# Two attentions dealt out pair by pair between weight products: a two-network kernel on one core

## The reference, cut to what matters

```python
h = rms_norm(x, norm_mix_pre[i])
z = h @ w_in[i]
c_q, c_kv, k_rope, q_c, k_c, v_c, g_a, g_b, g_c = jnp.split(z, split_points, axis=-1)
o_a = mla_attention(c_q, c_kv, k_rope, positions, ...)      # latent attention: 8 heads, all 512 keys
o_b = fourier_mix(h)
o_c = windowed_gqa(q_c, k_c, v_c, positions, gqa_sink[i])   # grouped: 8 heads, 3 key blocks of 128
merged = (jax.nn.sigmoid(g_a) * (o_a @ w_branch_a[i])
          + jax.nn.sigmoid(g_b) * (o_b @ w_branch_b[i])
          + jax.nn.sigmoid(g_c) * (o_c @ w_branch_c[i]))
x = x + rms_norm(merged @ w_out[i], norm_mix_post[i])
```

## Time and profile before

| | us |
|---|---|
| median of 3 runs (3287.8 to 3292.09) | 3291.27 |
| the profiled execution: time | 3288.2 |
| the profiled execution: span of its trace | 3286.4 |
| PE busy in the span | 3092.7 (94%) |
| DVE / ACT / POOL busy | 1221.0 / 1294.7 / 1495.4 |
| grouped attention, layer 0 and 1 | 51.3, 49.9 |
| latent attention, layer 0 and 1 | 70.3, 70.4 |

### The profile page before, as it was taken

One profiled execution on the slowest core, in us unless ns is written; L12 is line 12 of the kernel. 1 busy time (PEld: TensorE's weight loads), 2 busy tenths in 40 slices (PEclk: granted clock), 3 DMA queues, 4 the chain that ended last, 5 costly groups with the idle time before them and its releaser, 6 DMA issues.

```text
span 3286.4 us, 42020 instructions
## 1 busy us (share of the span) xinstructions
PE 3092.7 (94%) x15048; PEld 2487.2 (76%) x15048; DVE 1221.0 (37%) x2009; ACT 1294.7 (39%) x2023; POOL 1495.4 (46%) x879
## 2 busy tenths in 40 slices
PE   8989998999989989998999989879999998899999
PEld 6856676888867856686888769757788886688887
DVE  5345433221053445434221060443455215645510
ACT  3353543322243353543223243454555326344421
POOL 3366444444444456355444453343444433344443
PEclk9999999999999999999999989989999998899999
DMA  3212132233322213032333312101332322223332
GB/s 124 90 46 89 40 103 83 95 96 96 103 84 84 90 36 99 21 121 77 96 97 102 100 61 101 64 1 52 95 97 96 94 92 74 74 91 97 97 93 90
DMA packets 78522, 274.37 MB, mean 83 GB/s; under 512 B 8504, under 2 KB 12216, under 8 KB 78400
## 3 DMA queue, kind: packets, MB, share of 16 engines
q1 hardware_dynamic: 74064, 266.05, 25.8%
q10 hardware_dynamic: 4336, 6.63, 0.6%
HBM read 270.54 MB, written 2.10 MB: 83 GB/s over the span
## 4 chain that ended last, share of the span: by engine, by line
PE 83%; DVE 7%; ACT 4%; issue 3%; POOL 2%; DMA 1%; DVEq 0%; ACTq 0%; SPq 0%; POOLq 0%
PE ps L583 24%; PE ps L584 23%; PE ps L585 23%; PE ps L810 2%; PE ps L820 2%; DVE HL L1583 1%; PE ps L841 1%; PE ps L944 1%; PE ps L945 1%; PE ps L946 1%; PE ps L659 1%; DVE ps L1572 1%; DVE X L1575 1%; POOL WLO L2026 1%; ACT SG L1269 1%
## 5 line engine op out<-in xcount | busy, mean ns | idle before, releaser
L2026 POOL TENSOR_TENSOR WLO<-WRAW,WHI 128x1024 fp32r<-128x1024 f32 x471 | 1139.2, 2422 | 1338.4 <-ACT WHI L1110 1337.6
L583 PE MATMUL ps<-HH,WHI 128*128 128x512 f32 x2288 | 905.4, 396 | 47.2 <-DVE HL L1583 23.5
L585 PE MATMUL ps<-HH,WLO 128*128 128x512 f32 x2288 | 898.4, 393 | 0.0
L584 PE MATMUL ps<-HL,WHI 128*128 128x512 f32 x2288 | 898.2, 393 | 0.0
L1110 ACT ACTIVATE WHI<-WRAW 128x1024 fp32r<-128x1024 f32 x471 | 494.7, 1052 | 400.8 <-DMA WRAW<-wall 400.8
L583 PEld LDWEIGHTS ps<-HH,WHI 128*128 128x128 f32 x2288 | 434.0, 190 | 155.9 <-POOL WLO L2026 21.9
L585 PEld LDWEIGHTS ps<-HH,WLO 128*128 128x128 f32 x2288 | 434.0, 190 | 92.4
L584 PEld LDWEIGHTS ps<-HL,WHI 128*128 128x128 f32 x2288 | 434.5, 190 | 88.1
L1920 DVE SCALAR_TENSOR_TENSOR ps<-U,COLS,ps 128x512 f32<-128x512 f32 x208 | 157.1, 755 | 154.0 <-ACT ps L1426 138.7
L1606 DVE TENSOR_TENSOR ACC<-ACC,SQ 128x512 f32<-128x512 f32 x80 | 73.9, 923 | 318.2 <-ACT SQ L1295 303.2
L583 PE MATMUL ps<-F2H,WHI 128*128 128x512 f32 x384 | 151.7, 395 | 0.0
(11 more groups left out here) (353 smaller groups left out, 4781.8 us busy)
## 6 DMA issues: line engine op xcount, KB each, us to landing
WRAW<-wall SPq DMA_DIRECT2D x502, 512.0 KB, 3.6
DFT<-dft ACTq DMA_DIRECT2D x4, 516.0 KB, 5.7
XROWS<-xin SPq DMA_DIRECT2D x2, 1024.0 KB, 7.0
y<-YROWS ACTq DMA_DIRECT2D x4, 512.0 KB, 2.6
PROWS<-pin ACTq DMA_DIRECT2D x2, 512.0 KB, 3.9
DIL<-dil ACTq DMA_DIRECT2D x1, 768.0 KB, 5.3
COLS<-cols ACTq DMA_DIRECT2D x1, 294.5 KB, 6.4
POSI<-posi SPq DMA_DIRECT2D x1, 256.0 KB, 11.4
```

What stands on the lines that cost most here:

```text
L583: pe.matmul(out_, WHI[w_at], x_hi, start=first, stop=False)
L584: pe.matmul(out_, WHI[w_at], x_lo, start=False, stop=False)
L585: return pe.matmul(out_, WLO[w_at], x_hi, start=False, stop=last)
L2026: pool.tensor_tensor(WLO[:, s, :], whole, WHI[:, s, :].bitcast(F32), ALU.subtract).then_inc(wt_lo, 1)
```

## The change

The two attentions are no longer stages that own PE. A "carried" attention is dealt out by a host stage: `fourier_branch` carries the grouped attention (it also begins the next `branch`), and `branch_mla`, in place of the three rounds of `branch`, carries the latent one. At step q the host makes the scores of pair q, the values of q-3 and the turning of q-2, and beside them one piece of its own products. Banks: three go to the host's tiles, one to the heads; both score tiles now use one pair of banks (4 and 5) for all q. The turned tiles have 4 places in place of 8. Heads of the first three groups are first copied raw (OCR, OAR) and split at the end. Gates in the two hosts use sigmoid(x) = (1 + tanh(x/2)) / 2, in a tile GT of their own.

```diff
+HOSTS = ("fourier_branch", "branch_mla")
     def bank(self, k):
+        if self.kind in HOSTS:
+            k %= BANKS - 1
         return (self.t0 + k) % BANKS
...
         def score_bank(st, q, c):
-            return ps[4 + c] if q % 2 == 0 else ps[st.bank(2 + c)]
+            return ps[4 + c] if carried(st) or q % 2 == 0 else ps[st.bank(2 + c)]
         def scores_free(st, q):
             name = "exp_ready" if st.mode == "mla" else "scores_read"
-            return S[name], st.at(name, 2 * (q - 2) + 2)
+            return S[name], st.at(name, 2 * (q - (1 if carried(st) else 2)) + 2)
...
+            def fourier_branch(st):                    # PE
+                att, after = st.att, st.proj
+                attention_ready(att)
+                for q in range(att.heads * ST + DEPTH + 1):
+                    n, odd = divmod(q, 2)
+                    if q < att.heads * ST:
+                        scores(att, q)
+                    if q > DEPTH:
+                        value_products(att, q - DEPTH - 1)
+                    if n < DT and not odd:
+                        tile_part(st, 2 * n, 3 * n, pair["H"], DT, 0, 2)
+                    if DEPTH <= q < att.heads * ST + DEPTH:
+                        turn(att, q - DEPTH)
+                    if n < DT and not odd:
+                        tile_part(st, 2 * n, 3 * n, pair["H"], DT, 2, DT)
+                    elif n < DT:
+                        mirrored(st, n)
+                    elif q == 2 * DT:
+                        tile_part(after, 0, 0, pair["H"], DT, 0, 3)
+                    elif q == 2 * DT + 1:
+                        tile_part(after, 0, 0, pair["H"], DT, 3, DT)
...
+            def branch_mla(st):                        # PE
+                att = st.att
+                attention_ready(att)
+                pe.wait_ge(S["operand_ready"], st.op + st.kt)
+                for q in range(att.heads * ST + DEPTH + 1):
+                    r, part_ = divmod(q, 3)
...
+                    if r < DT - 2 and part_ < 2:
+                        tile_part(st, 2 * r, 2 * r, pair["H"], DT, 4 * part_, 4 * part_ + 4)
+                    elif r < DT - 2:
+                        tile_part(st, 2 * r + 1, 2 * r + 1, pair[st.src], st.kt, 0, st.kt)
...
+            def branch_mla(st):                        # ACT
...
+                    if q < att.heads * ST:
+                        exponentials(att, q)
+                    if DEPTH <= q < att.heads * ST + DEPTH:
+                        turned_copies(att, q - DEPTH)
...
+                    if part_ == 0:
+                        split_of(st, 2 * r)
+                    if part_ == 1:
+                        act.wait_ge(bank_free[st.bank(2 * r)], st.use(2 * r) + 1)
+                        act.activation(GT[:, :], GT[:, :], ACT.Tanh, scale=0.5).then_inc(S["gate_ready"], 1)
+                    if part_ == 2:
+                        split_of(st, 2 * r + 1)
...
+            def fourier_branch(st):                    # POOL
...
+                for q in range(att.heads * ST + 1):
+                    if q:
+                        probs_scaled(att, q - 1)
+                    if q + 2 < att.heads * ST:
+                        bias_pair(att, q + 2)
+                    if q < st.units:
+                        remainder_of(st, q)
```

More of the change, by code:

```diff
@@ L270, in attention @@
                 "banded": {"scores_read": n, "bias_scaled": DIL_H, "bias_ready": DIL_H + DIFF_H, "lambda_applied": DIFF_H * ST, "group_copied": DIFF_H}}[mode]
-        return add("attention", tiles=8, per=per, mode=mode, heads=groups, out=out, **opt)
+        if host is None:
+            return add("attention", tiles=8, per=per, mode=mode, heads=groups, out=out, **opt)
+        host.att = add("carried", per=per, mode=mode, heads=groups, out=out, **opt)
     tables = add("tables1", per={"table_stepped": 16, "table_looked_up": 8})
@@ L666, in fourier @@
                 mm.then_inc(S["tokens_transformed"], 1)
-            def fourier_branch(st):
[L669 to L689, removed]
@@ L694, in body @@
                         if j % 2 == 0:
-                            tile(st, j, j, r, pair["H"], DT)
+                            if not (st.begun and j == 0):
+                                tile(st, j, j, r, pair["H"], DT)
                         else:
@@ L798, in attention, with scores @@
                     pe.wait_ge(S["exp_ready"], st.at("exp_ready", 0))
+            def scores(st, q):
+                g, t = pairs_of(st)[q]
+                a, b = spans(st.mode, t)
+                if not carried(st) and q == 1:
+                    for c in range(2):
+                        pe.wait_ge(bank_free[st.bank(2 + c)], st.use(2 + c))
+                if q >= (1 if carried(st) else 2):
+                    pe.wait_ge(*scores_free(st, q))
+                for c in range(2):
+                    qs, ks = score_operands(st, g, c, t)
+                    pe.matmul(score_bank(st, q, c)[:, 0:(b - a) * P], qs, ks, start=True, stop=True).then_inc(S["scores_ready"], 1)
@@ L799, in attention @@
+            def attention(st):
+                n_pairs = st.heads * ST
+                attention_ready(st)
                 for q in range(n_pairs + DEPTH + 1):
                     if q < n_pairs:
[L801 to L807, removed]
@@ L822, in attention @@
-                    if q > DEPTH:
[L823 to L839, removed]
-                                for c in range(2):
-                                    mm = pe.matmul(out_bank(st, g)[half(c), at], values(g, c, kt), pt[:, (2 * p + c) % TURNED, (kt - a) * P:(kt - a + 1) * P],
-                                                   start=kt == a, stop=kt == b - 1, skip_group_check=True)
-                        mm.then_inc(S["pair_multiplied"], 1)
@@ new lines, in attention, with tile_part @@
+                        scores(st, q)
+                    if DEPTH <= q < n_pairs + DEPTH:
+                        turn(st, q - DEPTH)
+                    if q > DEPTH:
+                        value_products(st, q - DEPTH - 1)
+            def tile_part(st, j, k, src, kt, i0, i1):
+                if i0 == 0:
+                    weights(st.unit(j))
+                    pe.wait_ge(bank_free[st.bank(k)], st.use(k))
+                for i in range(i0, i1):
+                    mm = part(st, j, k, src, i, i == 0, i == kt - 1)
+                if i1 == kt:
+                    mm.then_inc(unit_used, 1)
@@ new lines, in fourier_branch @@
+                for q in range(att.heads * ST + DEPTH + 1):
+                    n, odd = divmod(q, 2)
+                    if q < att.heads * ST:
+                        exponentials(att, q)
+                    if DEPTH <= q < att.heads * ST + DEPTH:
+                        turned_copies(att, q - DEPTH)
+                    if q < 2 * DT:
+                        split_of(st, q)
+                    if n < DT and not odd:
+                        act.wait_ge(bank_free[st.bank(3 * n)], st.use(3 * n) + 1)
+                        act.activation(GT[:, :], GT[:, :], ACT.Tanh, scale=0.5).then_inc(S["gate_ready"], 1)
+                    elif n < DT:
+                        k = 3 * n + 2
+                        act.wait_ge(unit_used, st.unit(2 * n + 1) + 1)
+                        if n >= 2:
+                            act.wait_ge(bank_free[st.bank(k - 7)], st.use(k - 7) + 1)
+                        act.activation(TM[:, n % 2, 0:UH], ps[st.bank(k)][:, 0:UH], ACT.Copy, scale=0.5).then_inc(bank_free[st.bank(k)], 1)
@@ new lines, in fourier_branch, with heads_hi @@
+                heads_hi(att, unit_used, st.unit(2 * DT - 1) + 1)
+            def heads_hi(att, done, at):
+                act.wait_ge(done, at)
+                for g in range(att.heads):
+                    if g < att.heads - 1:
+                        act.wait_ge(bank_free[att.made.heads_bank()], att.made.heads_use(g) + 1)
+                    else:
+                        act.wait_ge(S["pair_multiplied"], att.at("pair_multiplied", 4 * g + 4))
+                    x = raw_heads(att, g) if g < att.heads - 1 else out_bank(att, g)[:, :]
+                    act.activation(pair[att.out][0][:, g, :], x, ACT.Copy).then_inc(S["operand_hi_ready"], 1)
@@ L1251, in rope, with exponentials @@
                 act.activation(KA[MLA_NOPE:MLA_QK, :, :], src, ACT.Copy).then_inc(S["rope_keys_spread"], 1)
+            def exponentials(st, q):
+                mode = st.mode
+                g, t = pairs_of(st)[q]
+                a, b = spans(mode, t)
+                w, s = (b - a) * P, 2 * (q % 3)
+                act.wait_ge(S["neg_max_ready"], st.at("neg_max_ready", q + 1))
+                if mode == "mla" and q >= 3:
+                    act.wait_ge(S["probs_turned"], st.at("probs_turned", 2 * (q - 3) + 2))
+                for c in range(2):
+                    p = probs_at(st, q, c)
+                    x, w_, scale = {"mla": (score_bank(st, q, c), w, MLA_QK ** -0.5), "gqa": (p, w + 1, 1.0)}.get(mode, (p, w, 1.0))
```

(16 more changed lines are left out.)

433 lines of the change are left out of this document (265 added, 168 removed).

## The result

The changed kernel takes 3266.47 us (median of 4 runs, 3263.98 to 3268.25), the kernel before 3289.88 us beside it (4 runs, 3287.80 to 3292.09). The ratio is 0.9928, 95% interval 0.9911 to 0.9945: 23.4 us faster. The forecast was 14.3 us and 3277.0; the sign and the range held, the gain was forecast 9 us too small. The profiled execution took 3265.9 us, its span 3264.1 (3286.4 before).

A forecast was written before the change was run, and what follows sets the result against it. PE, busy nearly throughout, bounds the kernel; its idle and lower-clock time can be won. 51.5 - 8.8 mixing - 11.2 latents - 1.0 - 11.2 rope - 5.0 clock = 14.3 us, giving 3277.0 us, range 3262 to 3293.

The forecast's parts named there:

- The bound and the main term: Both attentions: they wait on their chains, not on engine work; hiding these wins PE 51.5 us at most.
- The slack of 2.2 us: Steady host steps: a pair's exponentials end 4.4 us after its scores begin, inside a 6.6 us step.
- Mixing: Both hosts: PE's float32r/float32 round trips cost 0.1 us each, 44 a layer, 8.8 us in all.
- Rival (a): Both hosts: round trips cost nothing and the lower clock a bit less than put; 3264 us, chance 0.2.
- the 6.0 of the account: PE's lower clock after the waits at both joints: 1.0 us at the latents, 5.0 at the end of `rope`.
- Joint one: Between last grouped values and latents' sum: PE stands 6.9 us without its gate tile, giving back 5.6 a layer, 11.2.
- The 1.0 us of lower clock: Behind the wait for the latents' sum: more work at half clock, 0.5 us a layer.
- Joint two: End of `rope`: first latent scores wait for DVE's last addition, 11.2 us exposed, plus 5.0 of lower clock.
- The latent half at nothing: Carrying the latent attention: 9.2 won less 5.6 wait, 2.5 clock and 1.8 mixing a layer.
- Rival (c): Host steps with a gate's product on DVE: DVE comes late and PE waits; slower, 3313 us, chance 0.1.
- The grouped half: Carrying the grouped attention in `fourier_branch`: forecast to gain 8.5 and 7.1 us in the two layers.

The follow-up runs named there:

- fine_mixing: The changed kernel with each latent step's products cut into four pieces dealt out between scores, values and turning; 3269.73 us.
- gate_behind: The changed kernel with the next `branch`'s first gate tile put back behind the grouped attention's last values; 3258.57 us.
- rope_cover2: The changed kernel with the latent host's first two product pieces issued ahead of the wait for the rotated heads; 3256.93 us.
- latent_stage: The changed kernel with the latent attention a stage of its own again, only the grouped one carried; 3266.32 us.
- dve_load: The changed kernel with three (layer 0) or six (layer 1) unneeded DVE products ahead of each latent pair's maximum; 3319.61 us.
- rope_cover1: The changed kernel with one latent host product piece issued ahead of the wait for the rotated heads; 3262.23 us.

## Why the prediction was right, and where it was off

**The bound and the main term: right.** Pairs cost PE what they cost without waits: 70.2 + 34.1 + 5.6 for the begun tile is 109.9, and the grouped host took 110.87. The latent step is 6.54 us where 6.6 was expected. The slack of 2.2 us in the one pair of score banks came out at 2.27.

**Mixing, 8.8 us: mis-sized, and the main reason for the miss.** The grouped host leaves 110.87 - 109.9 = 1.0 us for 26 round trips, 0.04 each (a difference of large numbers, so a rough one); `fine_mixing` has 0.04 at most. In the latent host it is nothing: scores, values and turning take 1.82 + 1.02 + 0.85 = 3.69 us between products (318.44 to 322.13), 3.82 when they follow one another; twelve products then take 2.85 instead of 2.76. The first product behind values is 0.1 us late, in the earlier trace rows as now, but a block of attention behind products is as much faster. The step that failed was to charge the start of one block to the switch, without asking what the same block costs behind its old neighbour. At 0.04 the term is 3.5 us, 5 less than on record. Rival (a), given a chance of 0.2, was nearly right in this, and its 3264 is the nearest of the times named. In part that is luck: it also took 4 us off the lower clock, which came out less than 1 us below the 6.0 of the account.

**Joint one, 11.2 us: right.** The sum's wait grew from 1.26 to 6.88, 5.6 a layer as told. The 1.0 us of lower clock beside it came out at 0.3: from the first sum to the second it takes 7.73 us in layer 0 (8.12 before) and 7.87 in layer 1 (7.22 before). `gate_behind` shows that the term is a real price: it brings back 7.9 us of the 11.2; the rest went, by its rows, to two uncovered turnings and a chain that doesn't end as much sooner.

**Joint two, 11.2 and 5.0 us: right.** The wait is 6.35 us where there was 0.67; the lower clock costs 2.4 in layer 0 and 2.5 in layer 1 (first steps of 6.97 and 7.11 us, 4.57 and 4.58 in `rope_cover2`) where 2.5 was put. `rope_cover2` removes both at a cost of 1.6 us and gains 4.8 a layer. In a sum 5.7 + 2.4 - 1.6 = 6.5; in the trace layer 0 from `rope` to the norm is 6.5 shorter and layer 1 is 5.8, of which 2 to 3 us are lost again elsewhere in that execution.

**The latent half at nothing: nearly right.** -0.7 a layer was forecast, +2 is in the trace, 0 in the medians of `latent_stage`. 9.2 - 5.7 - 2.4 = 1.1 without the mixing. What carrying the latent attention wins, the uncovered end of `rope` takes.

**Adding up.** The grouped half was forecast at 8.5 and 7.1 us and gave 10.9 and 8.8; the latent at -0.7 twice and gave 2.0 twice. Of these 9.5 us, 5 or more are the mixing, 0.7 the clock behind the first joint; up to 3 us can't be told from the drift between executions.

**Rival (c)** didn't occur. Its reason fell away: the successor of L1655 averages 0.76 us (L1787, eight in layer 1) and the one of the latent host 0.99 (L1833, six), where L1655 averaged 1.93. The traces show where they lie. Before, all 16 of L1655 ran while POOL was in a remainder, and each ended about 0.55 us after the remainder did; the 2.54 of the earlier trace rows is one of them. Now only two of 16 and two of 12 meet a remainder, and they still end 0.5 to 0.6 us after it; the others meet scalings by POOL and take 0.66 to 0.72 us. The POOL row of before, then one DVE product beside a scaling and one beside a remainder in the changed kernel:

```profile
169.85 2.39 POOL L2026 TENSOR_TENSOR WLO<-WRAW,WHI 128x1024 fp32r<-128x1024 f32 x1
...
153.81 1.58 POOL L2311 TENSOR_SCALAR SGX<-SGX,RS 128x384 f32<-128x384 f32 x2 [0.69 <-DVE RS L1966]
154.21 0.72 DVE L1787 SCALAR_TENSOR_TENSOR MG<-GT,MG 128x512 f32<-128x512 f32 x1
...
406.88 2.39 POOL L2220 TENSOR_TENSOR WLO<-WRAW,WHI 128x1024 fp32r<-128x1024 f32 x1 [6.38 <-ACT WHI L1200]
407.59 2.23 DVE L1833 SCALAR_TENSOR_TENSOR MG<-TM,MG 128x512 f32<-128x512 f32 x1
```

So the new order of work moved most products out from under the remainders, which the reasoning of (c) had not asked about. No run moved them back. And `dve_load` shows that the slack is of the size that it was said to be.

## What to carry to other kernels

When work is interleaved into a stage, look at what the stretch between two stages used to hide: here most of the second half's gain went into a chain (the rotated heads) that had had 50 us of cover and now had none. A tile that can be run anywhere belongs where the engine would stand, not where it already has something to do; putting such work in its place at the two joints brought 21 us, nearly as much again as the whole change. And a price for switching read at the first instruction behind a switch is only half a price: compare a whole step in both surroundings.

## What was not expected of the hardware

PE's clock after a wait doesn't follow the wait's length alone. In `dve_load` scores after waits of 2.20, 2.21 and 2.35 us took 3.13, 3.41 and 3.78 us, at or near the lower clock; after 1.38 and 1.46 us they took 1.98, at the full one. In `gate_behind` the sum took 1.02 us after a wait of 2.29, at full clock, and 1.83 after 6.88 in the changed kernel. In `rope_cover1` the same wait, 2.75 and 2.76 us, gave scores of 3.75 us in one layer and 2.14 in the other. And in the kernel before, where the two waits around the first sum are equal in both layers (1.26 and 1.37 us, 1.27 and 1.36), the clock was already down behind them in layer 0, while in layer 1 it fell only at about 1213.4 (0.61 from 1213 to 1215), with PE at work since 1212.3. A half-covered wait can thus cost as much in clock as an uncovered one.

A DVE product of two operands in SBUF (L1655, L1787, L1833) that overlapped one of POOL's remainders ended 0.5 to 0.6 us after the remainder, in all 20 cases; beside POOL's scalings it took 0.66 to 0.72 us. The scaled gate L1842, which reads one operand from PSUM, took 0.69 us at 406.87 beside the remainder of 406.88.

A round trip between float32r products and float32 blocks on PE costs 0.04 us at most (0.05 us for three in a steady step of `fine_mixing`), and 46 more table loads of 1.28 us on ACT cost nothing that can be measured here, where ACT has idle time to spare.
